# LayerNorm of a convolution kept feature-major: sums over chunks on VectorE in place of transposes on TensorE

## What is computed

```python
def _layernorm(x, g, b):
    mu = jnp.mean(xf, axis=-1, keepdims=True)
    var = jnp.mean(jnp.square(xf - mu), axis=-1, keepdims=True)
    y = (xf - mu) * lax.rsqrt(var + EPS)
    return (y * g + b)

u = glu_a * jax.nn.sigmoid(glu_b)
u = depthwise_conv(u, conv_w) + conv_b                # 1024 tokens x 1024 channels
u = jax.nn.silu(_layernorm(u, conv_ln_g, conv_ln_b))  # mean and variance over the channels
y_conv = (u * jax.nn.silu(z_conv)) @ w_conv_out
...
y = sigmoid(g_conv) * y_conv + sigmoid(g_att) * y_att # y_att from the gated attention output
```

## Time and profile before

| | |
|---|---|
| time, median of 3 runs | 2804.42 us (2803.48 to 2807.59) |
| profiled execution: its time | 2803.69 us |
| its span in the trace | 2801.9 us |
| PE busy | 2747.3 us, 98% |
| DVE busy | 1796.7 us, 64% |
| ACT busy | 1256.8 us, 45% |
| POOL busy | 461.8 us, 16% |

### The profile page before, as it was taken

One profiled execution on the slowest core, in us unless ns is written; L12 is line 12 of the kernel. 1 busy time (PEld: TensorE's weight loads), 2 busy tenths in 40 slices (PEclk: granted clock), 3 DMA queues, 4 the chain that ended last, 5 costly groups with the idle time before them and its releaser, 6 DMA issues.

```text
span 2801.9 us, 36759 instructions
## 1 busy us (share of the span) xinstructions
PE 2747.3 (98%) x14640; PEld 2302.6 (82%) x14640; DVE 1796.7 (64%) x2475; ACT 1256.8 (45%) x2019; POOL 461.8 (16%) x422
## 2 busy tenths in 40 slices
PE   8999999999999999999999999999999999999998
PEld 7977888788884888888889888878888778888898
DVE  3644888330546888888875978988895464110575
ACT  4334787231432777777766125454454433011101
POOL 1500232000011111111112000000001154221341
PEclk9999999999999999999999999999999999999999
DMA  4131000421218999999972130030211311111131
GB/s 138 36 147 45 31 1 1 165 90 39 90 61 297 396 396 396 396 396 396 396 273 87 57 118 33 20 117 27 97 33 43 117 50 46 46 46 39 52 143 61
DMA packets 141558, 379.70 MB, mean 136 GB/s; under 512 B 11935, under 2 KB 45217, under 8 KB 141260
## 3 DMA queue, kind: packets, MB, share of 16 engines
q1 hardware_dynamic: 126140, 325.22, 30.6%
q0 software_dynamic: 12512, 42.61, 4.8%
q10 hardware_dynamic: 2736, 9.50, 0.9%
HBM read 340.99 MB, written 35.26 MB: 134 GB/s over the span
## 4 chain that ended last, share of the span: by engine, by line
PE 72%; DVE 4%; ACT 2%; issue 1%; DMA 1%; POOL 0%; POOLq 0%; ACTq 0%; DVEq 0%
PE ps L2854 7%; PE ps L2855 7%; PE ps L2856 7%; PE ps L2841 6%; PE ps L2839 6%; PE ps L2840 6%; PE ps L2462 4%; PE ps L2934 3%; PE ps L2936 3%; PE ps L2935 3%; PE ps L2981 2%; PE ps L2476 2%; PE ps L2946 1%; PE ps L2948 1%; PE ps L2947 1%; PE ps L2966 1%
## 5 line engine op out<-in xcount | busy, mean ns | idle before, releaser
L2232 DVE SCALAR_TENSOR_TENSOR b_f<-b_f,small_f 128x1023 f32<-128x1023 f32 (+14 forms) x240 | 304.4, 1268 | 27.0 <-ACT small_f L1268 13.8
L2854 PE MATMUL ps<-x_f32r,w_f32r 128*128 128x512 f32 x480 | 187.5, 391 | 0.9 <-issue 0.8
L2856 PE MATMUL ps<-x_f32r,w_f32r 128*128 128x512 f32 x480 | 186.9, 389 | 0.0
L2840 PE MATMUL ps<-w_f32r,a_f32r 128*128 128x512 f32 x456 | 177.4, 389 | 0.0
L2855 PE MATMUL ps<-ht_f32r,w_f32r 128*128 128x512 f32 x416 | 161.9, 389 | 0.0
L2935 PE MATMUL ps<-w_f32r,a_f32r 128*128 128x512 f32 x384 | 149.9, 390 | 0.0
L2840 PE MATMUL ps<-x_f32r,a_f32r 128*128 128x512 f32 x312 | 121.4, 389 | 0.0
L1183 POOL TENSOR_TENSOR w_f32r<-w_f,w_f32r 128x2048 fp32r<-128x2048 f32 x23 | 111.1, 4828 | 1.9
L1268 ACT ACTIVATE x_f<-ps 128x512 f32<-128x512 f32 (+1 forms) x184 | 91.0, 533 | 44.7 <-PE ps L2462 21.0
L2462 PE MATMUL ps<-small_f 128*128 128x128 f32 x792 | 103.7, 275 | 6.8 <-DVEq L1917 3.3
L2854 PEld LDWEIGHTS ps<-x_f32r,w_f32r 128*128 128x128 f32 x480 | 90.1, 188 | 20.1 <-issue 1.5
(11 more groups left out here) (555 smaller groups left out, 7939.5 us busy)
## 6 DMA issues: line engine op xcount, KB each, us to landing
w_f<-in_w_exp_up SPq DMA_DIRECT2D x40, 1024.0 KB, 9.8
w_f<-in_w_exp_down SPq DMA_DIRECT2D x38, 1024.0 KB, 10.2
w_f<-in_w_exp_gate SPq DMA_DIRECT2D x36, 1024.0 KB, 8.6
x_f<-in_w_exp_gate SPq DMA_DIRECT2D x28, 1024.0 KB, 8.3
x_f<-in_w_exp_down SPq DMA_DIRECT2D x26, 1024.0 KB, 10.7
x_f<-in_w_exp_up SPq DMA_DIRECT2D x24, 1024.0 KB, 10.0
w_f<-in_w_in SPq DMA_DIRECT2D x22, 1024.0 KB, 5.0
w_f<-in_w_in SPq DMA_DIRECT2D x10, 2048.0 KB, 7.8
```

Source lines behind the costliest of these rows:

```text
L2232: ins = v.scalar_tensor_tensor(C_conv[k][:, d:S], U_conv[k][:, 0:S - d], cols[:, k, R_TAP + j:R_TAP + j + 1], C_conv[k][:, d:S], ALU.mult, ...
L2840: mm(o, x1, w2[:, k, c], start=False, stop=False)
L2854: mm(o, l1, r1, start=(k == 0), stop=False)
L2856: ins = mm(o, l2, r1, start=False, stop=(k == n - 1))
```

## The change

The LayerNorm no longer turns the data. Its sums over the 8 chunks are made by DVE in feature-major form, in units of 128 channels by 512 tokens (16 units, `LN_UNITS`, in the order of chunks 4, 5, 6, 0, 1, 2, 7, 3):

1. DVE adds the 8 chunks (14 additions) into `ln_sum`. PE multiplies by a matrix whose elements are all 1/1024 (`mean`, one float32 matmul of 128 x 512 for each half, on the kind of line L2476), so every partition holds the means.
2. DVE subtracts the mean from `C` in place (16 units, one PSUM operand), ACT squares each unit, DVE adds the squares (14 additions of two SBUF operands) into `ln_sum2`.
3. PE forms the variances (`var`): 8 float32 matmuls of 128 rows by 1 column. DVE adds epsilon, POOL takes the root of 128 x 8 in two instructions, behind its split of gt1.
4. PE spreads the roots over the partitions (`rstd`, 8 transposes); DVE multiplies `C` by them in place (16 units, one PSUM operand). Gain and bias go into ACT's Silu as scale and bias of the channel; these 16 Silus now stand behind the `gt` gates 4 to 11.

The `at`, `za` and `gt` work stands in a list, `LN_STEPS`, around these steps, with six of the `gt` in it. POOL now does its 16 `ht_rest` pieces as 4 and 12, with the load of the second half of the attention output in between. The spare transposes are gone. Some semaphores are renamed or joined (`affine`, `gate`, `halves`, ...), which moves no work.

```diff
-        at_at = {0: [0], 1: [1], 2: [2, 3], 3: [4, 5], 4: [6, 7]}
-        za_at = {0: [2], 1: [3], 3: [4], 4: [5], 5: [6], 6: [7]}
-
         GT = [(c, h) for c in (6, 7, 4, 5, 2, 3, 0, 1) for h in range(2)]
-        gt_at = {6: [0, 1], 7: [2], 8: [3]}
-        za_mul_at = {3: [0, 1], 4: [2, 3], 5: [4], 6: [5], 7: [6], 8: [7]}
+        LN_STEPS = [("za", 2), ("za", 3)] + [("at", u) for u in range(4)] + [("za", 4)]
+        LN_STEPS += [("at", u) for u in range(4, T)] + [("za", 5), ("mean", 0), ("mean", 1), ("za", 6), ("za", 7)]
+        LN_STEPS += [("gt", u) for u in range(4)] + [("var", 0), ("gt", 4), ("gt", 5), ("rstd", 0), ("rstd", 1)]
+        LN_UNITS = [(k, h) for k in (4, 5, 6, 0, 1, 2, 7, 3) for h in range(2)]
...
-            for t in range(T):
-                pool.wait_ge(sem("ln_var"), t + 1)
-                v = st[:, 16 + 2 * t + 1:16 + 2 * t + 2]
-                ch(nc.gpsimd.tensor_scalar(st[:, 32 + t:33 + t], v, 1.0, EPS, ALU.mult, ALU.add))
-                nc.gpsimd.tensor_tensor(st[:, 32 + t:33 + t], st[:, 32 + t:33 + t], half[:, 0:1], ALU.pow).then_inc(sem("ln_rstd"), 1)
-                if t == 0:
-                    pool.wait_ge(sem("att_out"), 16 * T)
-                    att_load(1)
-                if t < 4:
-                    ht_rest(4)
-                elif t == 4:
-                    split("gt3")
-            for name in split_order[10:split_order.index("wo0")]:
+            ht_rest(4)
+            pool.wait_ge(sem("att_out"), 16 * T)
+            att_load(1)
+            ht_rest(12)
+            for name in split_order[9:split_order.index("wo0")]:
                 split(name)
+                if name == "gt1":
+                    bk.read(pool, ("var", 0))
+                    for i in (0, 4):
+                        ins = nc.gpsimd.tensor_tensor(ln_r[:, i:i + 4], ln_v[:, i:i + 4], half[:, 0:4], ALU.pow)
+                    ins.then_inc(sem("ln_rstd"), 1)
...
+            def ln_square(n):
+                k, h = LN_UNITS[n]
+                c = slice(NB * h, NB * h + NB)
+                if n < 14:
+                    act.wait_ge(sem("ln_part"), n + 1)
+                else:
+                    bk.read(act, ("mean", h))
+                if n >= 4:
+                    act.wait_ge(sem("ln_add"), n - 3)
+                dst = ln_sum2[:, c] if n < 2 else ln_sq[n % 2]
+                nc.scalar.activation(dst, C[:, k, c], ACT.Square).then_inc(sem("ln_sq"), 1)
+
+            gate(2), gate(3)
+            for u in range(4):
+                att_copy(u)
+            gate(4)
+            for u in range(4, T):
+                att_copy(u)
+            gate(5)
+            for n in range(16):
+                ln_square(n)
+                if n in (3, 7):
+                    gate(6 + n // 7)
+                elif n in (10, 13):
+                    merge_gate(*GT[(n - 10) // 3])
+            merge_gate(*GT[2]), merge_gate(*GT[3])
...
+            for n, (k, h) in enumerate(LN_UNITS):
+                c_ = C[:, k, NB * h:NB * h + NB]
+                if n < 14:
+                    act.wait_ge(sem("ln_part"), 14 + n + 1)
+                else:
+                    bk.read(act, ("rstd", h))
+                nc.scalar.activation(c_, c_, ACT.Silu, scale=cols[:, k, R_LNG:R_LNG + 1], bias=cols[:, k, R_LNB:R_LNB + 1]).then_inc(sem("ln_silu"), 1)
...
-                    bs = st[:, 68:80].rearrange("p (j s) -> p j s", j=2)
-                    mv = st[:, 16 + 2 * t:18 + 2 * t]
-                    bb = [bk.wait(dve, ("c1", t, j)) for j in range(2)]
-                    for j in range(2):
-                        ins = v.bn_stats(bs[:, j, :], PS[:, bb[j], :])
-                    ch(ins)
-                    ch(v.bn_aggr(mv, st[:, 68:80]))
-                    v.sem_inc(sem("ln_var"), 1)
-                    dve.wait_ge(sem("ln_rstd"), t + 1)
-                    if t >= 2:
-                        bk.wait(dve, ("c2", t - 2, 1))
-                    for j in range(2):
-                        bk.done(v.tensor_scalar(HN[t % 2][:, NB * j:NB * j + NB], PS[:, bb[j], :], mv[:, 0:1], st[:, 32 + t:33 + t], ALU.subtract, ALU.mult), ("c1", t, j))
-                if t >= 1:
-                    for j in range(2):
-                        b = bk.wait(dve, ("c2", t - 1, j))
-                        c_ = C[:, 4 * j:4 * j + 4, tile(t - 1)]
-                        bk.done(v.tensor_tensor(c_, b4(b), gain(R_LNG, 4 * j, 4 * j + 4), ALU.mult), ("c2", t - 1, j))
-                        bk.read(dve, ("c2", t - 1, j))
-                        v.tensor_tensor(c_, c_, gain(R_LNB, 4 * j, 4 * j + 4), ALU.add).then_inc(sem("ln_aff"), 1)
-                for u in za_mul_at.get(t, []):
-                    c, h = ZA[u]
-                    bk.read(dve, ("za", c, h))
-                    bk.read(dve, ("at", 4 * h + 2)), bk.read(dve, ("at", 4 * h + 3))
-                    a = attT[:, c, NB * h:NB * h + NB]
-                    v.tensor_tensor(a, a, za_tmp[u], ALU.mult).then_inc(sem("za_used"), 1)
+            def att_gate(u):
+                c, h = ZA[u]
+                bk.read(dve, ("za", c, h))
+                bk.read(dve, ("at", 4 * h)), bk.read(dve, ("at", 4 * h + 1))
+                bk.read(dve, ("at", 4 * h + 2)), bk.read(dve, ("at", 4 * h + 3))
+                a = attT[:, c, NB * h:NB * h + NB]
+                v.tensor_tensor(a, a, za_tmp[u], ALU.mult).then_inc(sem("za_used"), 1)
+
+            def half_of(x, h):
+                return x[:, NB * h:NB * h + NB]
+
+            ch(v.tensor_scalar(ln_ones, ident, 0.0, 1.0 / D, ALU.mult, ALU.add))
+            bk.wait(dve, ("qkt", 0, T - 1, 1))
+            for n, (k, h) in enumerate(LN_UNITS[2:]):
+                if h == 0 and k < 4:
+                    dve.wait_ge(sem(f"x_tile{k}"), CHUNK_BACK)
+                acc = half_of(ln_sum, h)
+                one = half_of(C[:, LN_UNITS[0][0], :] if n < 2 else ln_sum, h)
+                ins = v.tensor_tensor(acc, one, half_of(C[:, k, :], h), ALU.add)
+                ch.count(ins)
+                dve.wait_ge(ch.sem, ch.n - 1)
+            dve.wait_ge(ch.sem, ch.n)
+            v.sem_inc(sem("ln_sum"), 1)
+            for u in range(6):
+                att_gate(u)
+            dve.wait_ge(sem("att_out"), 16 * T)
+            means = [bk.wait(dve, ("mean", h)) for h in range(2)]
+
+            def square_add(n):
+                dve.wait_ge(sem("ln_sq"), n + 1)
+                if n >= 4:
+                    dve.wait_ge(sem("ln_add"), n - 3)
+                acc = half_of(ln_sum2, n % 2)
+                v.tensor_tensor(acc, acc, ln_sq[n % 2], ALU.add).then_inc(sem("ln_add"), 1)
+
+            for n, (k, h) in enumerate(LN_UNITS):
+                a = half_of(C[:, k, :], h)
+                ins = v.tensor_tensor(a, a, PS[:, means[h], :], ALU.subtract)
+                if n < 14:
+                    ins.then_inc(sem("ln_part"), 1)
+                else:
+                    bk.done(ins, ("mean", h))
+                if n >= 4:
+                    square_add(n - 2)
+                if n == 11:
+                    att_gate(6)
+            square_add(14), square_add(15)
+            dve.wait_ge(sem("ln_add"), 14)
+            v.sem_inc(sem("ln_sum"), 1)
+            att_gate(7)
+            b = bk.wait(dve, ("var", 0))
+            bk.done(v.tensor_scalar(ln_v, PS[:, b, 0:T], EPS, None, ALU.add), ("var", 0))
+            dve.wait_ge(sem("ln_part"), 14)
+            bk.read(dve, ("mean", 0)), bk.read(dve, ("mean", 1))
+            for n, (k, h) in enumerate(LN_UNITS):
+                a = half_of(C[:, k, :], h)
+                b = bk.wait(dve, ("rstd", h))
+                ins = v.tensor_tensor(a, a, PS[:, b, :], ALU.mult)
...
-            for t in range(T + 1):
-                if t < T:
-                    for j in range(2):
-                        b = bk.begin(pe, ("c1", t, j))
-                        for k in range(4):
-                            ins = turn(PS[:, b, tile(k)], C[:, 4 * j + k, tile(t)])
-                        bk.end(ins, ("c1", t, j))
-                for u in at_at.get(t, []):
+            for kind, u in LN_STEPS:
+                if kind == "at":
                     pe.wait_ge(sem(f"att_in{u // 4}"), 16)
                     turns(("at", u), att_tok[:, u, :])
-                for u in za_at.get(t, []):
+                elif kind == "za":
                     gate(u)
-                for u in gt_at.get(t, []):
+                elif kind == "gt":
                     c, h = GT[u]
                     split_wait(f"gt{c // 2}")
                     pe.wait_ge(sem("ht_lo"), 2 * KC)
                     feature_major(("gt", c, h), f"gt{c // 2}", c % 2, h, ht_2)
-                if t >= 1:
-                    for j in range(2):
-                        bk.read(pe, ("c1", t - 1, j))
-                    if t == 2:
-                        spare_turns(("c2", 1, 0), 24)
-                    for j in range(2):
-                        turns(("c2", t - 1, j), HN[(t - 1) % 2][:, NB * j:NB * j + NB])
```

(16 more changed lines are left out.)

78 lines of the change are left out of this document (34 added, 44 removed).

## The result

| | before | after |
|---|---|---|
| time, median | 2804.67 us (2803.48 to 2807.59, 9 runs) | 2812.03 us (2808.77 to 2814.93, 9 runs) |
| profiled execution, its span | 2801.9 us | 2809.1 us |

The account below looks back on a forecast made before the run. The prediction took PE's issue order between the window attention and the first `ya` as the bound. Its terms, -18.7 + 4.2 + 6.1 + 1.7 + 0 = -6.7 us, gave 2797.7 us, with an 8-in-10 range of 2792.5 to 2802.2.

Parts of the forecast that it names:

- The two engines take turns: DVE's additions against POOL's remainders ahead of `za` 4: about six additions get in, each costing POOL 0.48 us.
- the part on `ht_lo`: At `za` 4 PE waits 6.1 us for POOL's eighth remainder of `HT`; bounds 3.2 and 7.0.
- rival B: At `za` 4 the remainders come on time, wait 3.2 us, clock stays full: 2793.1 to 2794.8 us; chance 0.10.
- 16.6 + 0.3 - 4.2: PE's work before the first `ya`: 152 transposes (16.6 us) and block entries (0.3) removed; `mean`, `rstd`, `var` (4.2) added.
- its 14.5: Net us less for PE to issue before the first `ya`: 18.7 removed, including 1.8 of `HN` waits, against 4.2 added.
- The wait for the squares: At `var`, PE waits 0 us for DVE's sum of squares; bounds -2.4 to +4.
- 18.9 + 8: DVE's work before `var`: 31 instructions in 18.9 us, plus about 8 us of additions waiting behind POOL's splits.
- Clock: In `za` 4, behind PE's wait, a lowered clock costs 1.7 us; bounds nothing and 3.4.
- D: At `var`, additions run only after POOL's last split; wait about 7 us, kernel slower, 2806.4 us; chance 0.07.
- The stated sign for "wrong": Wrong if PE waits under 4 or over 8 us at `za` 4, over 2 at `var`, or later work stops following PE.

Follow-up runs that it names:

- e1_paused: The changed kernel with POOL waiting for its own result after each remainder of `HT`; 2798.89 us, 0.998 of before.
- e9: e4 plus 24 spare transposes on PE ahead of `za` 4, in its wait for the remainders; 2793.11 us, 0.996 of before.
- e4: The changed kernel with only PE's order changed: `mean` behind the first `gt`, `var` behind the sixth, `rstd` behind the seventh; 2793.76 us, 0.9961 of before.
- e6: The changed kernel with POOL waiting for the last attention tile's store to land before its first remainder; 2804.77 us, 1.0006 of before.
- e11: e4 with `var` behind the fourth `gt` and `rstd` behind the sixth; 2807.40 us, 1.0014 of before.

## Why the prediction was wrong

**The step that failed** is "The two engines take turns", in the part on `ht_lo`. From two pairs in the trace of before it was carried over to a train of 14 additions against a train of 16 remainders, with the delay put on POOL. In fact POOL's train was never disturbed and DVE's second addition stood through it. The wait that the forecast computed became 3.1 us instead of 6.1 (rival B's value), and a wait that it didn't have, for the sum ahead of `mean`, became 17.0. The forecast put this term at nothing without a reason: it never asked when that sum would be ready; it named what POOL loses by the contention, not what DVE loses. e1_paused, in which the turns are really taken, is its world: wait 6.5 us for 6.1, 2798.9 us for 2797.7.

**The other terms, one by one.** e9 has no clock loss and nearly no wait: 113.4 less 0.5 and 0.9 of waits and 24 spare transposes (2.6) leaves 109.4 us of PE work in the stretch; before it is 124.2 less the waits of 1.9 = 122.3. That is 12.9 us less, for 16.6 + 0.3 - 4.2 = 12.7 forecast (its 14.5 counts 1.8 us of removed waits as well). Of the additions, `mean` took 1.3 us at full clock (1.7 forecast), `var` 1.7 (1.6), `rstd` 0.8 (0.9). The wait for the squares was rightly put at nothing: the sum of squares was ready at 2325.0 us, 6.3 before PE came to it, and 25.9 us behind the first subtraction, for 18.9 + 8 = 26.9 forecast. Beyond the bare instructions, one addition there stands behind a split (4.50 us for 0.60), and DVE waits 2.6 us for ScalarE's squares. Clock: 1.7 us forecast behind a wait; measured 1.6 behind the long one and none behind the short one in this profile (2.6 in e4, at half the clock behind the same wait: 115.1 - 3.1 - 109.4); in e1_paused 2.6, since 13 matmuls of `za` 4 follow one another at 0.43 us instead of 0.23.

**The balance.** 109.4 + 3.1 + 17.0 + 1.6 = 131.1 us for the measured 130.9; against 124.2 before, 6.7 us slower, which is the span's 7.2 less the 0.55 us by which the stretch begins later.

**Rivals.** D, the one that ended slower, had the right engine and the right kind of event (additions that only run behind POOL) at the wrong train: it looked at the squares and at the splits. The stated sign for "wrong", a wait at `za` 4 under 4 us, is what showed.

**The rule.** The Trainium skill (SBUF — State Buffer, section "SBUF: two separate sides") was cited for an exclusive lock held for a whole instruction. Nothing in these runs speaks against that. It was read as if the lock changed hands at each instruction's end, and 23.23 us over 17 of POOL's compute instructions show that to be wrong here. That section of the Trainium skill also says that the one that starts first gets the ports. Here DVE's addition was issued at 2254.41, ahead of POOL's first remainder at 2254.60, and still lost. POOL's DMA issue was under way at that moment, but e6 shows that it alone does not hold such an addition up. The measurement decides.

## What to carry to other kernels

Where two engines contend for SBUF with trains of instructions, ask for each of them what is late if it gets nothing until the other's train breaks, and put a consumer behind enough other work to bear that; moving `mean` behind 16 us of products, with `var` behind two `gt` more and `rstd` behind one more, turned a loss of 0.2% into a gain of 0.4% (e4); moving `mean` alone left a loss of 0.1% (e11), because the next consumer, `var`, then waited. If the turn-taking itself is wanted, make the longer train pause (a wait for its own result, 0.08 us here). When work is removed from the critical engine, recompute the arrival time of every operand that it waits for, also of those that the change itself introduces.
